# A macaron transformer block on one core: three plain units after each group of seven block products, and seven of eleven hidden chunks turned and split in the output stage

## The reference

```python
def swiglu(x, w_in, w_out):
    gate, up = jnp.split(x @ w_in, 2, axis=-1)
    return (jax.nn.silu(gate) * up) @ w_out

h = h + 0.5 * swiglu(rmsnorm(h, ffn1_norm[l]), ffn1_w_in[l], ffn1_w_out[l])
# a gated-MLP group and stick-breaking attention, then cross-attention
h = h + 0.5 * swiglu(rmsnorm(h, ffn2_norm[l]), ffn2_w_in[l], ffn2_w_out[l])
return rmsnorm(h, final_norm)
```

## Time and profile before

| | |
|---|---|
| median of 3 runs | 2129.9 us (2128.22 to 2129.93) |
| the profiled execution, its own time | 2127.3 us |
| its span, first to last instruction | 2125.4 us |
| PE busy | 2107.7 us, 99% |
| DVE busy | 1530.6 us, 72% |
| ACT busy | 1093.8 us, 51% |
| longest wait of PE in total | 9.5 us, 20 times, for `t_lo_part` of DVE, line 1335 |
| mean granted TensorE clock | 0.999 |

### The profile page before, as it was taken

The page is one execution under the profiler, slowest core; times in us unless marked ns, Lnnn a source line. Parts: engine busy times, 40 slices in busy tenths (PEclk is TensorE's granted clock), DMA queues, the critical chain, the costliest instruction groups (busy, mean ns, idle before and its releaser), DMA issues.

```text
span 2125.4 us, 27293 instructions
## 1 busy us (share of the span) xinstructions
PE 2107.7 (99%) x9405; PEld 1738.6 (82%) x9405; DVE 1530.6 (72%) x1647; ACT 1093.8 (51%) x1251; POOL 38.3 (2%) x50
## 2 busy tenths in 40 slices
PE   9999999999999999999999999999999999999998
PEld 7778888878888888888888888887888887888887
DVE  8989999984555576566565656569999999964444
ACT  7555555553444465456544545555555555543433
POOL 0000000000000030000000000000000000000000
PEclk9999999999999999999999999999999999999999
DMA  8676667676566676765487766576667666785554
GB/s 297 212 236 224 218 221 234 222 257 228 203 234 210 227 258 217 241 215 185 175 286 239 235 208 195 187 243 209 219 214 236 226 217 211 238 286 195 191 187 157
DMA packets 185317, 472.37 MB, mean 222 GB/s; under 512 B 17056, under 2 KB 67616, under 8 KB 185120
## 3 DMA queue, kind: packets, MB, share of 16 engines
q1 hardware_dynamic: 183088, 464.11, 65.3%
q0 software_dynamic: 1728, 6.82, 0.9%
q10 hardware_dynamic: 432, 0.53, 0.1%
HBM read 443.60 MB, written 27.79 MB: 222 GB/s over the span
## 4 chain that ended last, share of the span: by engine, by line
PE 60%; DVE 18%; issue 9%; DMA 9%; ACT 3%; DVEq 0%; ACTq 0%; SPq 0%; POOL 0%; POOLq 0%
PE acc L1875 18%; PE acc L1878 18%; PE acc L1877 18%; DMA raw<-in_ffn_w_in 9%; DVE w_lo L1190 8%; DVE t_raw L1319 2%; DVE raw L1315 2%; DVE t_raw L1314 2%; ACT w_hi L728 1%; DVE stage L1230 1%; PE acc L2035 1%; DVE t_raw L1323 1%; DVE stage L1297 1%; PE acc L1899 1%; PE acc L1898 1%
## 5 line engine op out<-in xcount | busy, mean ns | idle before, releaser
L1190 DVE TENSOR_TENSOR w_lo<-raw,w_hi 128x1024 fp32r<-128x1024 f32 x765 | 924.1, 1223 | 476.1 <-ACT w_hi L728 473.5
L728 ACT ACTIVATE w_hi<-raw 128x1024 fp32r<-128x1024 f32 x765 | 794.4, 1055 | 839.0 <-PE acc L1878 530.6
L1875 PE MATMUL acc<-w_hi,a_hi 128*128 128x512 f32 x744 | 290.0, 390 | 0.0
L1877 PE MATMUL acc<-w_lo,a_hi 128*128 128x512 f32 x744 | 289.6, 389 | 0.0
L1878 PE MATMUL acc<-w_hi,a_lo 128*128 128x512 f32 x744 | 289.5, 389 | 0.0
L1875 PE MATMUL acc<-w_hi,b_hi 128*128 128x512 f32 x576 | 225.6, 392 | 0.0
L1878 PE MATMUL acc<-w_hi,b_lo 128*128 128x512 f32 x576 | 224.2, 389 | 0.0
L1877 PE MATMUL acc<-w_lo,b_hi 128*128 128x512 f32 x576 | 224.2, 389 | 0.0
L1898 PE MATMUL acc<-w_hi,b_hi 128*128 128x512 f32 x460 | 179.0, 389 | 0.0
L1898 PE MATMUL acc<-w_hi,a_hi 128*128 128x512 f32 x460 | 179.0, 389 | 0.0
L1899 PE MATMUL acc<-w_lo,b_hi 128*128 128x512 f32 x460 | 178.9, 389 | 0.0
(11 more groups left out here) (276 smaller groups left out, 2645.0 us busy)
## 6 DMA issues: line engine op xcount, KB each, us to landing
raw<-in_ffn_w_in SPq DMA_DIRECT2D x349, 512.0 KB, 4.3
raw<-in_ffn_w_out SPq DMA_DIRECT2D x176, 512.0 KB, 4.3
raw<-in_w_mix_in SPq DMA_DIRECT2D x80, 512.0 KB, 4.4
raw<-in_w_ckv SPq DMA_DIRECT2D x64, 512.0 KB, 4.3
memq<-bounce SPq DMA_DIRECT2D x196, 128.0 KB, 3.4
bounce<-stage SPq DMA_DIRECT2D x37, 512.0 KB, 6.1
raw<-in_w_mix_out SPq DMA_DIRECT2D x32, 512.0 KB, 4.4
raw<-in_w_cq SPq DMA_DIRECT2D x32, 512.0 KB, 4.3
```

The lines of the kernel that those rows point to most:

```text
L728: eng.activation(w_hi[:, u % RING], raw[:, u % RING], ACT.Copy).then_inc(w_hi_done, 1)
L1190: eng.tensor_tensor(w_lo[:, u % RING], raw[:, u % RING], w_hi[:, u % RING].bitcast(f32), ALU.subtract).then_inc(w_lo_done, 1)
L1875: eng.matmul(dst, x_hi[:, rows], w_hi[:, slot, i], start=start and i == 0, stop=False)
L1877: eng.matmul(dst, x_hi[:, rows], w_lo[:, slot, i], start=False, stop=False)
```

## The change

`BETWEEN = 3` plain units follow each fast group, so the groups stand at positions 0, 5 and 10, the last plain unit of the gate stands ahead of the last group, and four plain units (12 to 15) stand behind it. The hidden chunks 4 to 9 (the fifth to the tenth) are no longer fetched, turned and split in pairs 5 to 10 but, with chunk 10, in the first block of the output stage, at its units 0, 3, 6, ... 18 (lo and hi one unit later). In pairs 5 to 10 `stage` is guarded by the landing of its send instead. Send and fetch move by a position. Matmuls, loads and splits are as many as before.

```diff
+BETWEEN = 3
...
-        order += [("fast", s), ("fast", s)] + plain[:2]
-        plain = plain[2:]
+        order += [("fast", s), ("fast", s)] + plain[:BETWEEN]
+        plain = plain[BETWEEN:]
...
-GATE_END = PAIR_ORDER.index((0, U8 - 1)) + 1
+GATE_END = FAST_END
...
-SEND_AT = 10
-FETCH_AT = 12
+SEND_AT = 9
+FETCH_AT = 13
+LATE_CHUNKS = range(DC, FJ)
+LATE_TURN_AT = [3 * i for i in range(FJ - DC)]
+LATE_FETCH_AT = [0] + [at + 5 for at in LATE_TURN_AT[:-1]]
...
+                for turned_here, pairs in ((True, (1, DC + 1)), (False, (DC + 1, FJ))):
+                            if p == FETCH_AT and turned_here:
...
-                    if u == U8 + 2:
-                        fetch(number(TURNS, hid, FJ - 1))
+                    if u in LATE_FETCH_AT:
+                        fetch(number(TURNS, hid, LATE_CHUNKS[LATE_FETCH_AT.index(u)]))
...
-                        split(base, j, FAST_AT[s] + 2, PAIR)
-                        split(base, j, FAST_AT[s] + 3, PAIR)
-                    for p in range(4 * FAST, PAIR - 3):
-                        split(base, j, p, PAIR)
+                        for p in range(FAST_AT[s] + 2, (FAST_AT + [PAIR - 3])[s + 1]):
+                            split(base, j, p, PAIR)
...
-                    fill_hi(turned, number(TURNS, hid) + j, hid_dst, src=stage4)
+                    if hid_dst is not None:
+                        fill_hi(turned, number(TURNS, hid) + j, hid_dst, src=stage4)
...
-                    eng.wait_ge(t_read, number(FILLS, hid) + j)
+                    if hi is not None:
+                        eng.wait_ge(t_read, number(FILLS, hid) + j)
+                    else:
+                        eng.wait_ge(sent, 16 * number(TURNS, hid) + 16 * j)
...
+                    if u in LATE_TURN_AT:
+                        c = LATE_CHUNKS[LATE_TURN_AT.index(u)]
+                        if u == 0:
+
+                            eng.wait_ge(gate_read, FJ * (1 + TURNED.index(hid)))
+                        turn_fill(hid, c, number(TURNS, hid, c))
+                    if u - 1 in LATE_TURN_AT:
+                        c = LATE_CHUNKS[LATE_TURN_AT.index(u - 1)]
+                        fill_lo(split_number(hid, c), hid_lo[:, 4 * c - KT:4 * c - KT + 4],
+                                hid_hi[:, 4 * c - KT:4 * c - KT + 4])
```

More of the change, by code:

```diff
@@ L512, in ffn_in @@
                     chunk(w, U8, base + U8, before=last)
[L513 to L519, removed]
+                for turned_here, pairs in ((True, (1, DC + 1)), (False, (DC + 1, FJ))):
+                    with eng.Fori(*pairs) as j:
+                        for p in range(PAIR):
+                            if p == SEND_AT:
+                                send(number(TURNS, hid) - 1 + j, stage[:], hid_done, silus[base] + j)
+                            if p == FETCH_AT and turned_here:
+                                fetch(number(TURNS, hid) - 1 + j, first=base == FFN1_IN)
+                            load(w, PAIR * j + p, base + PAIR * j, p)
             def h_again(in_base, q):
@@ L852, in ffn_in @@
                 with eng.Fori(DC + 1, FJ) as j:
-                    pair(j, hid_hi[:, bass.ds(4 * j - 4 - KT, 4), :])
+                    pair(j, None)
             def ffn_out(base, hid, name, h_hi, gain):
@@ L1342, in pair @@
                         fast_lo(j, s)
[L1343 to L1349, removed]
+                        for p in range(FAST_AT[s] + 2, (FAST_AT + [PAIR - 3])[s + 1]):
+                            unit_lo(j, p)
+                            if p == FAST_AT[0] + 2:
+                                up_drained(j - 1)
+                    if hi is not None:
+                        turn(number(TURNS, hid) - 1 + j, stage4)
                     eng.wait_ge(p1_copied, done)
                     eng.tensor_tensor(shared[:, 0], sum_p6, copy_p1, ALU.add).then_inc(p6_added, 1)
-                    fill_lo(split_number(hid) - 1 + j, lo, hi, src=stage4)
+                    if hi is not None:
+                        fill_lo(split_number(hid) - 1 + j, lo, hi, src=stage4)
                     unit_lo(j, PAIR - 3)
@@ L1376, in ffn_in @@
                 with eng.Fori(DC + 1, FJ) as j:
[L1377 to L1378 removed]
+                    pair(j, None, None)
                 return up_drained, hidden
@@ L1925, in fast @@
                     three(sum_p6, s2, sum_block(1), start, stop)
-                    three(acc[:, 1], block_of(UK * s + 1, 1), sum_block(2), start, False).then_inc(t_used, 1)
+                    three(acc[:, 1], block_of(UK * s + 1, 1), sum_block(2), start, stop).then_inc(t_used, 1)
                     eng.wait_ge(w_lo_done, unit + 2)
-                    three(acc[:, 0], block_of(UK * s + 1, 0), ring_block(p + 1, 0), start, False)
+                    three(acc[:, 0], block_of(UK * s + 1, 0), ring_block(p + 1, 0), start, stop)
                     if s == 0:
@@ L1967, in ffn_out @@
                 eng.wait_ge(gate_read, silus[in_base] + FJ)
-                eng.wait_ge(t_read, number(FILLS, hid, FJ - 2) + 1)
                 for u in range(U22):
-                    if u == U22 - 2:
-                        eng.wait_ge(t_read, number(FILLS, hid, FJ - 1) + 1)
+                    if u == 0 or UK * u % 4 == 0 and UK * u // 4 in LATE_CHUNKS:
+                        eng.wait_ge(t_read, number(FILLS, hid, UK * u // 4 if u else DC - 1) + 1)
                     unit(0, u, 0)
```

14 lines of the change are left out of this document (6 added, 8 removed).

## The result

| | before | after |
|---|---|---|
| median | 2129.06 us (2128.21 to 2129.93, 4 runs) | 2190.05 us (2189.28 to 2192.57, 4 runs) |
| ratio of the two | | 1.0289, 95% interval 1.0274 to 1.0305 |
| the profiled execution | 2127.3 us, span 2125.4 | 2192.57 us, span 2190.4 |

The changed kernel is 2.9% slower, 61 us; 2179 us was predicted, with a range to 2201. The kernel before has one run more here than in the table ahead of the prediction. The changed kernel's profiled run is the slowest of its four, so the profile shows 65 us more span where the medians differ by 61.

The account below looks back on a forecast made before the run. PE was taken to bound the kernel, busy 2107.7 of 2125.4 us. Tails 33.6 + 29.3 + 1.4, group 1 4.3, less 18.2 of removed waits, gave +50.4 us: 2179 us, range 2165 to 2201.

Parts of the forecast that it names:

- The tails: Behind each pair's last group: PE loses 4.20 us in pairs 1 to 4, 2.93 in 5 to 9, 0.7 in 10.
- T + 16.28 and T + 15.01: End of `t_lo_part` in pairs 1 to 4 and 5 to 9, from PE's possible start behind the last group, T.
- Group 2, "count nothing": Sums of group 2 in each pair: chain of 12.1 to 13.4 us against PE's 12.92, short end taken, no loss.
- Group 1, 0.24 us in 18 pairs: Group 1's chain through position 6's load: 0.08 us late, 0.24 with restart, 4.3 us in all; 16 at 4.7 us load.
- The output stage, "off the path, I count nothing": Late turns and splits in the output stage's first block: DVE needs at most 54.2 of 59.8 us, so no loss.
- The price I gave for a failed cover: Output stage, units 8 to 20: PE waits up to about 1 us at each of seven chunks, 14 us for both FFNs.
- Rival 3: The output stage starves, with fetches, loads and residual reload in flight together: 14 us on top, 2193 us; chance 3%.
- my list of signs that the prediction is wrong: Pairs of about 41.5 us, PE waits in the output stage, clock below 9, or `t_lo_part` well before T + 15.
- rival 4: Clock halves after waits in 20 tails, at most 2.7 us each, 54 us: about 2233 us; chance 3%.
- All else of the 18.2 us goes: PE's present waits for `t_lo_part` in the pairs, 18.2 us over both FFNs, vanish except for group 1's loss.
- The sum: Whole kernel: 33.6 + 29.3 + 1.4 + 4.3 - 18.2 = +50.4 us, forecast 2179 us, 2.3% slower.

Follow-up runs that it names:

- splits_early: Changed kernel with splits of positions 13, 14 and the hidden chunk ahead of ACT's copy and DVE's first gate addition, ACT's 15 ahead of SiLU: 2136.38 us, ratio 1.0049.
- drain_first: Changed kernel with DVE's drain of the up half ahead of the split of position 2 instead of behind it: 2196.44 us, ratio 1.0327.
- send_early: Kernel before the change, with only the hidden chunk's send moved ahead of the load of position 8: 2129.46 us, ratio 1.0015.
- late_send_early: `late_only` with the hidden chunk's send two loads earlier, ahead of the load of position 8: 2117.79 us, ratio 0.9961.
- late_only: Changed kernel with the old order of two plain units between groups, keeping the late chunks in the output stage: 2118.75 us, ratio 0.9963.
- reload_late: Changed kernel with the four residual reloads at units 12 to 15 of the output stage instead of 4 to 7: 2184.74 us, ratio 1.0271.
- late_send: `late_only` with the hidden chunk's send one load later, behind the load of position 10: 2137.92 us, ratio 1.0046.

## Why the prediction was right, and where its terms were off

- **The tails** were right. The chain of the earlier trace rows was forecast to end at T + 16.28 and T + 15.01 and ended at T + 16.25 and T + 14.98; the losses of 4.20, 2.93 and 0.7 us measured 4.17, 2.90 and 0.7, so the terms 33.6 + 29.3 + 1.4 = 64.3 us come to 63.8 over the whole tails, and 62.1 by the stops alone. `splits_early` shows that this chain is the cost. The pairs lasted 44.6 to 45.3 us in pairs 5 to 9 and 45.7 to 47.6 in pairs 2 to 4, about as forecast.
- **Group 2, "count nothing"**, was right: one loss of 1.33 us in twenty pairs, where the load of position 11 took 6.1 us; in the others it took 4.0 to 5.0. (Its long end was 20 x 0.56 = 11 us, not 12.)
- **Group 1, 0.24 us in 18 pairs**, was undersized: 8.4 us, 0 to 1.02 per pair, within the 16 us of its upper bound. The chain is right and the load's duration was the term that was off: the step took one load of 4.0 us, and the twenty take 3.4 to 4.9, with the loss going up as they do (and 3.4 to 3.6 in `drain_first`). Its pieces add up to 13.12 us and not 13.16, which makes the term 3.6 us and not 4.3. The Trainium skill, "DMA: Bandwidth & Descriptors", section on the anatomy of one DMA, gives an estimate of 3.2 us by its sum for this size. The page fits that sum to transfers issued by GpSimd, and the loads here are issued by SP, which the prediction did not say. Loads with the most room around them come near it (3.3 us at the least), all others are longer; the measurement decides.
- **The output stage, "off the path, I count nothing"**, failed: 8.3 us. The step added up DVE's work (54 of 60 us) and left out that its turns wait for fetches. SP was said to have no other work than waiting for `w_lo`; it also reloads the residual there. DVE idles 4.66 us in one turn, and two things on SP make that wait: the reloads ahead of the fetch, and the late start of the stage's loads and fetches behind the tail of pair 10. The price I gave for a failed cover, up to 1 us at each of seven chunks, 14 us, was over the 8.3 measured and not right in kind: it came as two long waits, one per FFN. Rival 3 had this with a chance of 3%, too low. Waits of PE in the output stage were also on my list of signs that the prediction is wrong.
- **The clock** (rival 4) fell once, at 1950.7, within the stop of 3.24 us, and not in the tails, whose waits reach 1.45 us. There the rival's price, 2.7 us for the matmuls of one unit, was about right: 6.1 less 3.24 leaves 2.9. The Trainium skill, "TensorE: Matmul & The Clock Gate", section on why this matters for kernels, warns that idle gaps bring the clock back to half. The stop of 3.24 us agrees; after the waits in the tails the trace shows no such fall, and of the stops of about 2 us in the output stages of these kernels one was followed by it and three were not.
- **"All else of the 18.2 us goes"** was nearly right: the losses of group 2 went. But it read them as the work of the load of position 9, which holds for 12 of the 18 us. `send_early` and `late_send_early` cured that load, and the loss moved to the other groups, since DVE needs 11.08 us between groups 0 and 1 where PE has 10.20.
- **The sum** of +50.4 us would be +62.8 with the terms measured by stops (62.1 + 8.4 + 1.4 + 1 + 8.3 - 18.4), where the span of the profiled run gives 65.0 and the medians 61. The miss of some 11 us is mainly the output stage (8.3 where nothing was counted) and group 1 (8.4 for 4.3). That the time lies in the range owes little to errors that cancel: only the tails were too high, by 0.5 to 2 us.

What stays open: why a load takes from 3.4 to 4.9 us in pairs that issue the same transfers. How much of the gain of `late_only` is DVE's time, ACT's or the fetches'. And whether the lead of the fetch is all that makes the late chunks starve the output stage in the new order and hardly in the old one: it is read from the traces, and no run moved it alone.

## What to carry to other kernels

When work is moved from behind a step to between steps, time the chain that begins at that step against what is left to cover it, from its first instruction to the one that releases the critical engine; here 18 repetitions of 2.8 to 4.1 us far outweighed the 18 us of waits that the move removed. Before a load is eased because PE waits for it, check whether the loss merely moves: an edit that takes work out of the loop helped, three that only shifted the send did not. (Shifting the reload in the output stage did help, where PE waited for the transfer behind it.) An engine with idle time to spare is no cover for a moved step until what the step waits for, and what is queued ahead of it on the DMA queue, has been costed too.

## What the runs showed of the hardware

- **The clock after a stop.** Behind one stop of 3.24 us PE's matmuls stood 0.427 us apart instead of 0.227 until 1957.4 (granted clock 0.57 in that stretch of 5 us). Some seventy shorter waits, up to 1.45 us in the tails, left the clock at 1.00. The length of the stop alone does not tell: in `drain_first` a stop of 1.95 us at 1953.9 was followed by the lower level from 1956.3 to 1959.7 (0.66 from 1955 to 1960), while stops of 1.96 us in `reload_late`, 2.10 us in the changed kernel and 2.20 us in FFN 1 of `drain_first` left it at 1.00.
- **A 512 KB load has no fixed duration.** It took 3.3 to 3.6 us with room around it, 3.4 to 4.9 at position 6 with a neighbour close by, 4.7 to 6.6 at position 9 of the kernel before, with a send right behind it (5.3 in the earlier trace rows), and 6.5 to 12.7 among reloads and fetches in the output stage (the five issued from 1934.4 to 1943.8). Behind a split delayed by 1.13 us the sums that needed the load were only 0.65 us later.
- **A queue in order.** A fetch that waits on SP for a send holds up the loads behind it, the first of them by about 2.8 us in pair 3 of `late_send`, where the send took 5.88 us to land; moving the send by one position cost 18 us in all.
